# A two-layer mixture-of-experts trunk: last expert's rows weighted in their one-hots, residual of two tiles added on TensorE, last down product by halves

## What is computed

```
for layer in range(2):
    x = x + mixer(rms_norm(x))            # layer 0: HGRN2 + differential attention, layer 1: gated linear attention
    h = rms_norm(x)
    for e in range(16):                   # each token has weights for two experts only
        y = y + combine[:, e:e+1] * ((silu(h @ w_gate[e]) * (h @ w_up[e])) @ w_down[e])
    x = x + y
```

## Time and profile before

| what | value |
|---|---|
| runs | 1241.45, 1241.93, 1246.71 us, median 1241.93 |
| the profiled execution's own time | 1237.31 us |
| its span | 1235.4 us |
| mean granted clock of TensorE | 0.982 |
| TensorE busy | 1163.7 us, 94% |
| VectorE busy | 905.0 us, 73% |
| ScalarE busy | 670.8 us, 54% |

### The profile page before, as it was taken

The page is one execution under the profiler, slowest core; times in us unless marked ns, Lnnn a source line. Parts: engine busy times, 40 slices in busy tenths (PEclk is TensorE's granted clock), DMA queues, the critical chain, the costliest instruction groups (busy, mean ns, idle before and its releaser), DMA issues.

```text
span 1235.4 us, 16987 instructions
## 1 busy us (share of the span) xinstructions
PE 1163.7 (94%) x5804; PEld 886.3 (72%) x5804; DVE 905.0 (73%) x1253; ACT 670.8 (54%) x841; POOL 199.4 (16%) x158
## 2 busy tenths in 40 slices
PE   6999979989999999999978999998999999999996
PEld 5776668878866777777646788887886677777763
DVE  5556768575589888888866247656568988888887
ACT  4444541124267788888743332132336778887872
POOL 1220000010022233223230000001002223322323
PEclk9999999999899999999989999999989999999999
DMA  6241110131699999999850150113169999999956
GB/s 230 94 114 46 68 69 1 69 137 69 269 338 388 389 393 399 397 394 393 318 190 12 61 156 3 68 68 136 69 247 344 387 385 393 399 398 393 394 224 218
DMA packets 96655, 281.76 MB, mean 228 GB/s; under 512 B 18944, under 2 KB 19456, under 8 KB 96592
## 3 DMA queue, kind: packets, MB, share of 16 engines
q1 hardware_dynamic: 87056, 247.51, 53.3%
q0 software_dynamic: 5888, 20.97, 5.4%
q10 hardware_dynamic: 3648, 12.45, 2.6%
HBM read 262.05 MB, written 18.87 MB: 227 GB/s over the span
## 4 chain that ended last, share of the span: by engine, by line
PE 73%; DVE 16%; ACT 4%; issue 3%; DMA 1%; POOL 1%; DVEq 0%; ACTq 0%; POOLq 0%; SPq 0%
PE PS L1155 21%; PE PS L1157 21%; PE PS L1156 20%; DVE expert_w_low L1925 3%; PE PS L1260 3%; DVE group_low L1755 2%; PE PS L1442 2%; PE PS L1194 1%; PE PS L1371 1%; DVE AT L1855 1%; PE PS L1413 1%; DVE G L1576 1%; DVE x_sb L1630 1%; DVE hT_low L1739 1%; ACT prob L1046 1%
## 5 line engine op out<-in xcount | busy, mean ns | idle before, releaser
L1925 DVE TENSOR_TENSOR expert_w_low<-expert_w,weight_high 128x1024 fp32r<-128x1024 f32 x338 | 410.4, 1266 | 68.5 <-ACT weight_high L917 57.9
L917 ACT ACTIVATE weight_high<-expert_w 128x1024 fp32r<-128x1024 f32 x384 | 375.1, 1048 | 57.4 <-PE PS L1157 49.5
L1155 PE MATMUL PS<-weight_high,xgT_high 128*96 128x512 f32 x512 | 204.4, 399 | 2.9 <-DVEq L1935 2.9
L1157 PE MATMUL PS<-weight_high,xgT_low 128*96 128x512 f32 x512 | 203.2, 397 | 0.0
L1156 PE MATMUL PS<-expert_w_low,xgT_high 128*96 128x512 f32 x512 | 202.1, 395 | 0.0
L1155 PE MATMUL PS<-group_high,hT_high 128*128 128x512 f32 x416 | 170.7, 410 | 5.9 <-DVEq L1741 3.0
L1157 PE MATMUL PS<-group_high,hT_low 128*128 128x512 f32 x416 | 163.9, 394 | 0.0
L1156 PE MATMUL PS<-group_low,hT_high 128*128 128x512 f32 x416 | 163.4, 393 | 0.0
L1755 DVE TENSOR_TENSOR group_low<-group_w,group_high 128x1024 fp32r<-128x1024 f32 x68 | 80.7, 1222 | 48.0 <-ACT group_high L941 44.1
L1155 PE MATMUL PS<-weight_high,actT_high 128*96 128x512 f32 x256 | 103.4, 404 | 8.8 <-DVEq L1983 8.8
L1155 PEld LDWEIGHTS PS<-weight_high,xgT_high 128*96 128x96 f32 x512 | 83.3, 163 | 36.3 <-DVEq L1935 3.0
(11 more groups left out here) (258 smaller groups left out, 1575.2 us busy)
## 6 DMA issues: line engine op xcount, KB each, us to landing
expert_w<-in_moe_w_gate SPq DMA_DIRECT2D x32, 2048.0 KB, 13.4
expert_w<-in_moe_w_up SPq DMA_DIRECT2D x32, 2048.0 KB, 13.5
expert_w<-in_moe_w_down SPq DMA_DIRECT2D x32, 2048.0 KB, 13.6
group_w<-in_even_w_in SPq DMA_DIRECT2D x6, 2048.0 KB, 7.9
group_w<-in_odd_w_in SPq DMA_DIRECT2D x6, 2048.0 KB, 8.6
y_rows<-yb ACTq DMA_DIRECT2D x30, 384.0 KB, 6.1
group_w<-in_even_w_out SPq DMA_DIRECT2D x2, 2048.0 KB, 7.7
h_rows<-h SPq DMA_DIRECT2D x8, 512.0 KB, 10.3
```

Source lines behind the costliest of these rows:

```text
L917: act_(hi, w, ACT.Copy).then_inc(w_hi, 1)
L1155: pe.matmul(out, ah, bh, start=first, stop=False)
L1157: return pe.matmul(out, al, bh, start=False, stop=final)
L1925: tt(lo, w, hi.bitcast(F32), ALU.subtract).then_inc(w_lo, 1)
```

## The change

- The one-hots of the last expert carry `w_last` in place of the assignment, so the row products come out weighted. For tiles 0 and 1 `add_last` becomes a plain tensor_tensor of PSUM and x.
- For tiles 2 and 3 TensorE puts x itself into the banks with an identity matrix (`residual`: two f32 matmuls of 128*128 by 128x512 for a tile), tile 2 ahead of the last expert's transposes of `act`, tile 3 behind them. Their row products add to it. VectorE's first gathered add of these tiles takes PSUM in place of x, and their `add_last` is gone.
- The last down product goes column half by column half; ScalarE copies the first half during the second.
- The row products have four pairs of banks (6 and 7, 2 and 3, 4 and 5, 0 and 1) and are no longer tied to the adds in the list of steps: three stand at its beginning, the fourth behind the first transposes. Layer 1's first projection takes banks 2 to 5.
- The order of the steps changes: `mean[1]` ahead of `low[2]`, `low[3]` behind `h[1]`, the two adds of tile 2 on either side of `hT[1]`, the adds of tile 3 together.
- In the overflow part, which isn't entered here, the banks of the residual are closed at the start and filled again at the end.

```diff
@@ -210,18 +210,28 @@
...
-        return [x[0], x[1], p[0], high[0], low[0], stat[0], mean[0], high[1], h[0], p[1], high[2], high[3], hT[0], low[1],
-                stat[1], low[2], mean[1], low[3], halves[0], h[1], x[2], p[2], hT[1], stat[2], mean[2], u[0], halves[1], h[2],
-                x[3], p[3], hT[2], stat[3], mean[3], u[1], halves[2], h[3], hT[3], u[2], halves[3], u[3]]
-
-    sums = [[("x", 0), ("x", 1), ("p", 0), ("p", 1), ("x", 2), ("p", 2), ("x", 3), ("p", 3)],
-            [("x", 0), ("x", 1), ("x", 2), ("p", 0), ("p", 1), ("x", 3), ("p", 2), ("p", 3)]]
...
+        rows = [("last", n, i) for i in range(NT)]
+        x = [[("x", n, i, c) for c in range(2)] for i in range(NT)]
+        return [*x[0], *x[1], *rows[0:3], p[0], high[0], low[0], stat[0], mean[0], high[1], h[0], p[1], high[2], high[3],
+                hT[0], rows[3], low[1], stat[1], mean[1], low[2], halves[0], h[1], low[3], x[2][0], hT[1], x[2][1],
+                stat[2], mean[2], u[0], halves[1], h[2], *x[3], hT[2], stat[3], mean[3], u[1], halves[2], h[3], hT[3],
+                u[2], halves[3], u[3]]
+
+    in_loop = [s for s in norm_steps(2) if s[0] in ("x", "p")]
+    sums = [[(s[0], *s[2:]) for s in in_loop],
+            [("x", 0, 0), ("x", 0, 1), ("x", 1, 0), ("x", 1, 1), ("p", 0), ("p", 1),
+             ("x", 2, 0), ("x", 2, 1), ("x", 3, 0), ("x", 3, 1)]]
+    PER_LAYER = NT + len(in_loop)
...
         def unit_bank(s):
+            if s[1] == 1 and s[2] == "v":
+                return s[3] + 2
...
             for i in range(NT):
-                bk.plan(("P", l, i), ([2, 3], [4, 5])[i % 2])
+                bk.plan(("P", l, i), ([6, 7], [2, 3], [4, 5], [0, 1])[i])
...
                     key = ("down", l)
                     if last:
-                        bk.wait_full(sc, key, b)
                         for c in range(2):
+                            if c == 0:
+                                sc.wait_ge(last_half, l + 1)
+                            else:
+                                bk.wait_full(sc, key, b)
                             link(act_(y_last[0:CAP, c * GC:(c + 1) * GC], PS[0:CAP, 2 + c], ACT.Copy))
                             sc.sem_inc(y_ready, 1)
                         sc.sem_inc(bk.freed(key), 1)
...
+            def residual(l, i, start=True, stop=False):
+
+                for c in range(2):
+                    pe.matmul(PS[:, bk.uses[("P", l, i)][0] + c], ident[:], x[:, i, c * GC:(c + 1) * GC], start=start, stop=stop)
...
                 key = ("P", l, i)
                 if i == 0:
                     pe.wait_ge(bk.freed(("lastT", l)), bk.uses[("lastT", l)][1])
-                bk.acquire(pe, key)
+                if i < 2:
...
                 for c in range(2):
                     if i == 0:
                         pe.wait_ge(y_ready, 2 * l + c + 1)
                     ins = pe.matmul(PS[:, bk.uses[key][0] + c], lastT[:, i * P:(i + 1) * P],
-                                    y_last[0:CAP, c * GC:(c + 1) * GC], start=True, stop=True)
+                                    y_last[0:CAP, c * GC:(c + 1) * GC], start=i < 2, stop=True)
...
                     if last:
+
+                        bk.acquire(pe, ("P", l, 2))
+                        residual(l, 2)
                         act_T(b)
+                        bk.acquire(pe, ("P", l, 3))
+                        residual(l, 3)
...
-                    for k in range(DE // P):
-                        wait_low(p0, b0, k)
-                        for c in range(2):
-                            ins = three(PS[0:CAP, 2 + c], ((actTh[:, k], actTl[:, k]),
-                                                           (hi[:, 2 * k + c], lo[:, 2 * k + c])),
-                                        k == 0, k == DE // P - 1)
+                    steps = [(k, c) for k in range(DE // P) for c in range(2)]
+                    if last:
+                        steps = [(k, c) for c in range(2) for k in range(DE // P)]
+                    for n, (k, c) in enumerate(steps):
+                        if c == 0:
+                            wait_low(p0, b0, k)
+                        ins = three(PS[0:CAP, 2 + c], ((actTh[:, k], actTl[:, k]),
+                                                       (hi[:, 2 * k + c], lo[:, 2 * k + c])),
+                                    k == 0, k == DE // P - 1)
+                        if last and n == DE // P - 1:
+                            ins.then_inc(last_half, 1)
...
                 with pe.If(more > 0):
+
+                    for i in (2, 3):
+                        residual(l, i, False, True)
...
                         pe.wait_ge(ov_act[l], b * 4 + 4)
-            for kind, i in sums[NL - 1]:
-                if kind == "p":
-                    rows_of_last(NL - 1, i)
+                    for i in (2, 3):
+                        residual(l, i)
+            for i in range(NT):
+                rows_of_last(NL - 1, i)
...
+            def add_gathered(l, i, c):
+
+                k, key = 2 * i + c, ("P", l, i)
+                w = rt["wt"][:, c, i:i + 1]
+                ve.wait_ge(yg_sem[k], 16 * (l + 1))
+                if c:
+                    ve.wait_ge(x_new, x_count(l, "x", i, 0))
+                if i >= 2 and c:
+                    ve.sem_inc(bk.freed(key), 1)
+                if i >= 2 and c == 0:
+
+                    bk.wait_full(ve, key)
+                    b = bk.uses[key][0]
+                    stt(by_bank(x[:, i]), by_bank(yg[k][:]), w, PS[:, b:b + 2], ALU.mult, ALU.add).then_inc(x_new, 1)
+                else:
+                    stt(x[:, i], yg[k][:], w, x[:, i], ALU.mult, ALU.add).then_inc(x_new, 1)
 
             def add_last(l, i):
 
                 key = ("P", l, i)
                 bk.wait_full(ve, key)
-                ve.wait_ge(x_new, x_count(l, "x", i))
-                xs = x[:, i].rearrange("p (c n) -> p c n", c=2)
+                ve.wait_ge(x_new, x_count(l, "x", i, 1))
                 b = bk.uses[key][0]
-                link(stt(xs, PS[:, b:b + 2], rt["w_last"][:, i:i + 1], xs, ALU.mult, ALU.add))
+                link(tt(by_bank(x[:, i]), PS[:, b:b + 2], by_bank(x[:, i]), ALU.add))
...
                 for i in range(NT):
-                    ins = ts(ohj[:, i], iota_f[:, 0:CAP], rank[:, i, NE - 1:NE], r["M"][:, i, NE - 1:NE], ALU.is_equal, ALU.mult)
+                    ins = ts(ohj[:, i], iota_f[:, 0:CAP], rank[:, i, NE - 1:NE], r["w_last"][:, i:i + 1], ALU.is_equal, ALU.mult)
```

More of the change, by code:

```diff
@@ L212, in norm_steps, with x_count, x_final @@
         p = [("p", n, i) for i in range(NT)]
[L213 to L224 removed]
+        rows = [("last", n, i) for i in range(NT)]
[9 more added lines that the diff above has]
+    PER_LAYER = NT + len(in_loop)
+    def x_count(l, *what):
+        if what[0] == "wo":
+            return PER_LAYER * l + what[1] + 1
+        return PER_LAYER * l + NT + sums[l].index(what) + 1
+    def x_final(l, i):
+        return x_count(l, "p", i) if i < 2 else x_count(l, "x", i, 1)
     def with_splits(l, steps):
@@ L1195, in _ @@
                             ins.then_inc(bk.filled(k), 1)
-                    elif kind == "p":
+                    elif kind == "last":
                         rows_of_last(l - 1, s[2])
@@ L1612, in constants, with by_bank @@
                     link(ts(nth[:, c], it, float(c + 1 - NG), None, ALU.add))
-            def add_gathered(l, i):
-                for c in range(2):
-                    k = 2 * i + c
-                    ve.wait_ge(yg_sem[k], 16 * (l + 1))
-                    if c:
-                        ve.wait_ge(x_new, x_count(l, "x", i) - 1)
-                    stt(x[:, i], yg[k][:], rt["wt"][:, c, i:i + 1], x[:, i], ALU.mult, ALU.add).then_inc(x_new, 1)
+            def by_bank(a):
+                return a.rearrange("p (c n) -> p c n", c=2)
+            def add_gathered(l, i, c):
[12 more added lines that the diff above has]
+                    stt(x[:, i], yg[k][:], w, x[:, i], ALU.mult, ALU.add).then_inc(x_new, 1)
             def add_last(l, i):
@@ L2055, in _ @@
                         tt(act[0:CAP], PS[0:CAP, 1, :], ex[0:CAP], ALU.mult).then_inc(ov_ve[l], 1)
-            for kind, i in sums[NL - 1]:
-                (add_gathered if kind == "x" else add_last)(NL - 1, i)
+            for kind, *which in sums[NL - 1]:
+                (add_gathered if kind == "x" else add_last)(NL - 1, *which)
 _INS = ['x', 'attn_norm', 'ffn_norm', 'even_w_in', 'even_w_out', 'hg_lb_logits', 'hg_o_norm', 'da_q_norm',
```

15 lines of the change are left out of this document (6 added, 9 removed).

## The result

The median of the changed kernel is 1235.9 us (five runs, 1230.5 to 1240.0) against 1241.9 (five runs, 1240.4 to 1247.5): 6.0 us less. The ratio estimated from all these runs, which is not the quotient of the two medians, is 0.9944, with a 95% interval of 0.9917 to 0.9971: 7 us less, with an interval from 3.6 to 10. The forecast was 3.65 us less (1238.3, range 1233.5 to 1243.0). The profiled execution took 1230.49 us (before: 1237.31).

What follows compares the result with a forecast made beforehand. The prediction took VectorE's work at the layer boundary and in layer 1's tail to bound what the change touches. It summed -2.65 and -1.0 to -3.65 us against the median 1241.93, giving 1238.3 us, range 1233.5 to 1243.0.

Steps and rivals of the forecast that it cites:

- Rival 2: Gain above forecast: free TensorE branch, 1.1 us more in the tail, total -4.75; fewer half-clock stretches, -6.3 to -7.9; chance 0.15.
- Residual, +0.45 a layer: Around the last expert's transposes of act: f32 identity matmuls overrun their holes and delay the down product 0.45 us.
- Weights in the one-hots, 0: Last expert's one-hots and adds of tiles 0 and 1: same cost, 0, bounds -0.1 and +0.1 us each.
- The clock, -1.55 in layer 0: Layer 0's last down product: filling the hole before it keeps the clock from falling, saving 1.55 us.
- Branch on TensorE, -0.4: After the last down product: load and branch hold row products 1.2 us after its end, 1.55 before, saving 0.4.
- Tail, -1.0: Layer 1 after its last expert: VectorE's last add starts at 1229.9 instead of 1230.93, 1.0 us sooner.
- Boundary, -2.65: Between layer 0's experts and layer 1's first projection: last transposes start at 664.7 instead of 667.34, 2.65 us sooner.
- The new hole: Layer boundary, VectorE: tile 2's square, mean and root follow its second add with nothing beside them, 2.33 us.
- Rival 1: Layer boundary: clock still falls in layer 0's down product or after the opened hole; total -0.7 to -2.3; chance 0.20.
- Rival 3: Layer 1's first projection: long half-clock stretch makes the kernel slower, total +1.2 us, 1243.1, or 1248; chance 0.08.
- rival 4: VectorE at the layer boundary: the removed adds were hidden anyway, leaving -2.4 us, 1239.5; chance 0.05.

Runs made afterwards that it cites:

- experiment 3: Kernel before with four f32 identity matmuls a layer filling the last expert's two holes, written to banks nobody reads; one run, 1240.14 us.
- experiment 4: Kernel before with four pairs of banks for the row products and the projection's banks moved, nothing else; one run, 1238.10 us.
- experiment 5: Changed kernel with both adds of tile 2 ahead of the transposes of tile 1; one run, 1236.92 us.
- the repetition: Changed kernel with both adds of tile 2 ahead of tile 1's transposes, timed again beside the unaltered changed kernel; median 1232.67 us, ratio 0.9933 to before.
- experiment 2: Changed kernel without the residual matmuls, tiles 2 and 3 having their add of the last expert's rows back on VectorE; twelve runs, ratio 0.9986 to before.
- the second profile: Changed kernel, unaltered, profiled and timed once more; median 1235.99 us, ratio 0.9959 to before.

## Why the prediction was right, and by what it fell short

The sign, the range and the two places were right; the size was 5.6 us at these places for 3.65. Rival 2's first half, with its 4.75, comes nearest. Step by step:

- *Residual, +0.45 a layer.* 0.29 (0.28 in experiment 3). The records cost 0.43 us as taken, but the first down matmul was not late at all; the second was, by 0.28.
- *Weights in the one-hots, 0.* The adds of tiles 0 and 1 take 1.22 us in place of 1.28, 0.06 less each, within the bound.
- *The clock, -1.55 in layer 0.* It stayed up, in this kernel and in experiment 3. But the add of tile 0 then waited for its gather, as the working had it, so it bought little. An estimate: in layer 1, where no gather held it, the add started 11.63 us after U; with the 1.56 us that the fall cost (10.62 less 9.06) that makes 13.2, and the gathers let it start no sooner than 13.67 and 13.18 in the two profiles. The hole was followed by a fall in two of six cases, and filled it was followed by none in twenty (two in each of ten profiles). That the filled ones merely met the chip at another moment is not the reason in all of them. In the kernel before and in experiment 4 the clock fell 4.8 us after U, and again 18.4 to 18.5 us after U, about the first transposes. In experiment 5 and its repetition, which have the filled hole, it also fell 18.5 us after U, so its changes lay alike there, but it did not fall at 4.8:

```profile
626.20:631.90 5.70, 5.70 (x25) 3.87 (x24) 2.26 (x2) 0.59 (x1) 4.17 (x6) 1.00 0.88 289
641.00:644.40 3.40, 3.40 (x9) 1.85 (x8) 2.65 (x4) 2.31 (x5) 0.00 (x0) 0.50 0.00 0
```

  These are windows of the repetition (U at 622.56). The Trainium skill, "TensorE: Matmul & The Clock Gate", Part 1, has the chip look at times of its own; unlike outcomes of the same hole (1.00 in experiment 2, 0.75 before, over the down product) agree.
- *Branch on TensorE, -0.4.* **This term failed.** The text took ScalarE's 1.19 us for TensorE's load and branch. The row products follow 0.23 us behind the last down matmul: the branch costs nothing there, and the whole 1.72 us was to be had, 1.3 more than counted. The rule of the Trainium skill, "Runtime: NRT & Kernel Launch", Instruction fetch mechanics, on taken branches, set beside it, would have made the gain 0; no row shows such a stall on TensorE, although the skipped part had grown. This was rival 2's first half (-1.1 in the tail). Why ScalarE stands idle and TensorE does not is not shown. On ScalarE the register load starts at 635.0 in the kernel before, 0.2 us behind the end of its last copy (634.81), and the branch follows at 635.75; of TensorE's load and branch the trace has no record.
- *Tail, -1.0.* -2.48. From the first row product to the last add's start I had 9.7 us, and it was 9.72; the miss is the branch term and 0.16 of the residual.
- *Boundary, -2.65.* -3.14, by two errors. The gathers let the add of tile 0 gain 0.90 instead of 1.37 (by them, the add starts between 12.0 and 13.8 us after U). The way from there shrank by 2.24 instead of 1.28. Of these 0.96 us a third lies ahead of the new hole, where VectorE's instructions followed each other directly and I had put 0.1 us and more between them. A third is the hole itself: 2.03 us from the end of tile 2's second add to its h, where I took tile 0's 2.33. A third lies in the adds and low parts behind it, again closer together than written. Half clock behind the first transposes cost both profiles about 0.5, so it is not a part of this difference; the second profile, without it, has a way of 27.61.
- *The new hole.* 1.9 us of idle time (2.3 forecast) and on the path, as forecast: closing it took 1.2 us off (experiment 5). The clock did not fall behind it here; it did in experiment 2.
- *Rival 1* (the clock gives nothing back, or falls behind the new hole) did not come in either profile of the changed kernel. *Rival 3* (a long stretch at half clock there) did not come in any profile, *rival 4* is refuted by experiment 2. The parts do not add up, since they share waits: in the tail the residual is worth 2.22 us and the halves 0.91, together more than the 2.48 of the whole change.

## What to carry to other kernels

Price a wait for its releaser and for what stands ready behind it: here the freeing of a bank was named on TensorE, behind it stood a copy (1.22 us, experiment 4), and behind that nothing, not even the branch (0.23 us). An idle time of one engine around a branch is no price for another. When adds are moved, look what ran beside them: the change saved two adds and laid bare a square, a mean and a root that had been covered. And read differences of a few microseconds as distances from a common event, not as times of runs.

## What was not expected of the hardware

Thirteen executions of kernels with the same code up to there reached U in layer 0 anywhere from 622.2 to 628.2 us. Added up over windows of 2 us, the granted clock was at its lower level for 17 us of the first 620 in the four that got there by 622.51, and for 24 to 31 us in the seven that took until 625.4 or longer; the remaining two (622.6 and 623.9) had 20. Layer 1 adds as much: from the last transposes of the boundary to U in layer 1 the same thirteen took from 540.9 to 547.2 us, with 10 us at the lower level in the shortest and 27 in the longest. The two do not go together: the repetition of experiment 5 reached the first U 5.7 us before experiment 5 did, and ended only 2.0 us sooner. So, by and large, the longer a layer ran at the lower clock, the later it ended, and each layer's spread of some 6 us is as large as the effect that was to be measured (the changed kernel's runs lie between 1230 and 1242 us).
